# A two-block transformer kernel: the distance of moving tiles from the weights, a narrow panel turned round, and sums of squares token by token

## What is computed

```python
# first block, per layer
h = x @ w_in                       # 12 parts: q, k, v, gates, latents
cq, ckv = rmsnorm(b_cq), rmsnorm(b_ckv)
yc = rmsnorm(diff_attention(...))  # 4 heads of 128: a mean of squares per head and token
merged = ga * (ya @ w_a) + gb * (yb @ w_b) + gc * (yc @ w_c)
r = ALPHA * x + merged @ w_o
r = r + sigmoid(r @ w_pg) * (p_i @ w_p)
x = layernorm(r)
# second block, per layer
u = modulate(rmsnorm(h));  h += gate * swiglu(u, wg, wu, wd)      # width 2816
u = modulate(rmsnorm(h));  proj = u @ w_in                        # 5128 columns
# the last 8 columns of proj are mdt: dt = softplus(mdt + dt_bias), one per head of mamba
h += gate * (concat(retention, stick_breaking, mamba2) @ w_out)
u = modulate(rmsnorm(h));  h += gate * swiglu(u, ...)
```

## Time and profile before

| | |
|---|---|
| median of 3 runs | 2003.1 us (2002.36 to 2005.24) |
| the profiled execution | 2002.46 us, its span 2001.2 us |
| PE busy | 1893.1 us, 95%, 14952 matmul records |
| DVE busy | 1372.0 us, 69% |
| ACT busy | 954.4 us, 48% |
| mean granted TensorE clock | 0.978 |
| read from HBM | 386 MB, 194 GB/s over the span |

### The profile page before, as it was taken

One profiled execution on the slowest core, in us unless ns is written; L12 is line 12 of the kernel. 1 busy time (PEld: TensorE's weight loads), 2 busy tenths in 40 slices (PEclk: granted clock), 3 DMA queues, 4 the chain that ended last, 5 costly groups with the idle time before them and its releaser, 6 DMA issues.

```text
span 2001.2 us, 34162 instructions
## 1 busy us (share of the span) xinstructions
PE 1893.1 (95%) x14952; PEld 1819.0 (91%) x14952; DVE 1372.0 (69%) x1955; ACT 954.4 (48%) x1318; POOL 63.3 (3%) x76
## 2 busy tenths in 40 slices
PE   7998988899899898999999999999999999999998
PEld 7987888899788887999999889999999999799998
DVE  5667676666766767776775867767777776866555
ACT  5564454455644545434455435445444446344443
POOL 0000100000001001000000000001000000010000
PEclk9999999989999998999999999999999999999999
DMA  7453446464453554666455344665665455335551
GB/s 302 171 200 148 159 184 222 182 234 153 184 190 116 224 212 169 254 243 239 185 196 221 117 163 179 251 245 240 241 256 239 163 218 208 129 141 190 180 179 63
DMA packets 59285, 389.70 MB, mean 195 GB/s; under 512 B 6656, under 2 KB 9472, under 8 KB 15232
## 3 DMA queue, kind: packets, MB, share of 16 engines
q1 hardware_dynamic: 59136, 387.52, 50.6%
HBM read 386.45 MB, written 1.05 MB: 194 GB/s over the span
## 4 chain that ended last, share of the span: by engine, by line
PE 67%; DVE 21%; ACT 10%; issue 1%; DMA 0%; POOL 0%; SPq 0%; DVEq 0%; ACTq 0%
PE banks L753 17%; PE banks L754 16%; PE banks L755 16%; DVE weights_split L905 7%; PE bank L755 4%; PE bank L754 4%; PE bank L753 4%; ACT weights_split L899 4%; ACT map L1340 1%; DVE weights L885 1%; DVE xbc L2297 1%; DVE map_stat L1528 1%; ACT map L1346 1%; PE bank L820 1%; PE bank L831 1%
## 5 line engine op out<-in xcount | busy, mean ns | idle before, releaser
L905 DVE TENSOR_TENSOR weights_split<-weights,weights_split 128x2048 fp32r<-128x2048 f32 (+2 forms) x306 | 656.8, 2148 | 337.8 <-ACT weights_split L899 337.1
L753 PE MATMUL banks<-u,weights_split 128*128 128x258 f32 (+1 forms) x2016 | 578.3, 287 | 17.2 <-DVE weights_split L905 6.6
L899 ACT CAST weights_split<-weights 128x2048 fp32r<-128x2048 f32 (+2 forms) x306 | 542.5, 1775 | 80.2 <-PE bank L755 50.6
L754 PE MATMUL banks<-u,weights_split 128*128 128x258 f32 (+1 forms) x2016 | 575.6, 286 | 0.0
L755 PE MATMUL banks<-u,weights_split 128*128 128x258 f32 (+1 forms) x2016 | 572.5, 284 | 0.0
L753 PEld LDWEIGHTS banks<-u,weights_split 128*128 128x128 f32 x2016 | 384.6, 191 | 21.6 <-DVE weights_split L905 8.2
L755 PEld LDWEIGHTS banks<-u,weights_split 128*128 128x128 f32 x2016 | 387.9, 192 | 0.0
L754 PEld LDWEIGHTS banks<-u,weights_split 128*128 128x128 f32 x2016 | 386.3, 192 | 0.5 <-issue 0.5
L753 PE MATMUL banks<-x,weights_split 128*128 128x256 f32 x1056 | 302.9, 287 | 15.0 <-DVE weights_split L905 9.8
L754 PE MATMUL banks<-x,weights_split 128*128 128x256 f32 x1056 | 297.0, 281 | 0.0
L755 PE MATMUL banks<-x,weights_split 128*128 128x256 f32 x1056 | 296.9, 281 | 0.0
(11 more groups left out here) (320 smaller groups left out, 2561.1 us busy)
## 6 DMA issues: line engine op xcount, KB each, us to landing
weights<-in_weights SPq DMA_DIRECT2D x262, 1024.0 KB, 6.9
weights<-in_ada SPq DMA_DIRECT2D x80, 1024.0 KB, 4.8
weights<-in_weights SPq DMA_DIRECT2D x36, 512.0 KB, 5.5
weights<-in_weights SPq DMA_DIRECT2D x4, 576.0 KB, 5.3
constants_second<-in_constants_second SPq DMA_DIRECT2D x1, 1792.0 KB, 9.9
weights<-in_weights SPq DMA_DIRECT2D x2, 640.0 KB, 7.5
h<-in_x SPq DMA_DIRECT2D x2, 512.0 KB, 5.1
out<-xbc SPq DMA_DIRECT2D x4, 256.0 KB, 2.1
```

The costliest lines, as they stand in the source:

```text
L753: pe.matmul(out, left[0], right[0], start=start, stop=False, **more)
L754: pe.matmul(out, left[0], right[1], start=False, stop=False, **more)
L899: act.do.copy(split[:, 0, 0:n], raw[:, 0:n]).then_inc(*self.act_wrote.inc(("weights", key)))
L905: dve.do.tensor_tensor(split[:, 1, 0:n], raw[:, 0:n], split[:, 0, 0:n].bitcast(F32), ALU.subtract).then_inc(*self.dve_wrote.inc(("weights" ...
```

## The change

Three things are changed. First, a tile `space` of 128 bytes is put behind the split buffers, and the rows of `u` are made 384 elements (1536 bytes) long, of which 258 are used; the scratch for DMA descriptors shrinks from 16384 to 1024 bytes. Second, in `m_dt` the 8 columns of the panel are the stationary side and the 256 tokens move; ACT copies the 8 rows to SBUF, PE transposes them token-major (`turn_dt`) behind the first `s_q` panel, and `steps` comes after that. Third, the sums of squares are made token-major: the squares are stationary and one column of ones moves, so that each sum stands in its own row; DVE needs one small operation for all of them in place of the reduces, and the Newton step has one operation less.

```diff
+U_ROW = 384
@@ order of the mixers
         self.run(self.dense("m_dt", l, [0]))
-        self.add("steps", l)
...
         filler = Filler(fill())
+        filler.step()
+        self.add("turn_dt", l)
+        self.add("steps", l)
         filler.until("stick-breaking can start")
@@ tiles
         self.split = self.new_ring([self.tile(f"weights_split{i}", [P, 2, SLOT], F32R) for i in range(SPLIT_SLOTS)])
+        self.tile("space", [P, 32])
...
-        b["u_shift"] = sb("u", [P, DC, 2, T + 2], F32R)
-        b["u"] = b["u_shift"][:, :, :, 0:T]
+        u = sb("u", [P, DC, 2, U_ROW], F32R)
+        b["u_shift"], b["u"] = u[:, :, :, 0:T + 2], u[:, :, :, 0:T]
...
+        b["dt_rows"] = b["m_z"][0:MH, 0, :]
@@ tensor_norm
-            for g in range(0, groups, 2):
-                sums, some = ring.take(("sums", tag, g)), min(2, groups - g)
-                pe.wait_ge(*ring.free(("sums", tag, g)))
-                for k in range(chunks):
-                    pe.wait_ge(*wrote[k])
-                    rhs = squares[:, k, :] if groups == 1 else self.two(squares[:, g:g + 2, :])
-                    last = pe.do.matmul(sums[:, 0:some * T], self.k("ones"), rhs, start=k == 0, stop=k == chunks - 1)
-                last.then_inc(*self.filled.inc(("sums", tag, g)))
+            sums = ring.take(("sums", tag, 0))
+            pe.wait_ge(*ring.free(("sums", tag, 0)))
+            for k in range(chunks):
+                pe.wait_ge(*wrote[k])
+                for g in range(groups):
+                    for t in range(TB):
+                        col, square = g * TB + t, squares[:, g if groups > 1 else k, t * P:(t + 1) * P]
+                        last = pe.do.matmul(sums[:, col:col + 1], square, self.k("ones")[:, 0:1],
...
+            last.then_inc(*self.filled.inc(("sums", tag, 0)))
@@ vector_norm
-                dve.do.tensor_tensor_reduce(
-                    self.diagonal, sums[:, i * P:(i + 1) * P], self.k("ident"), 1.0 / count, eps, ALU.mult, ALU.add,
-                    mean[:, col:col + 1]).then_inc(*self.dve_wrote.inc(("mean", tag, g)))
...
+        dve.do.tensor_scalar(mean, ring.tile(("sums", tag, 0))[:, 0:n], 1.0 / count, eps, ALU.mult, ALU.add).then_inc(
+            *self.dve_wrote.inc(("mean", tag)))
...
-        dve.do.tensor_tensor(tmp, mean, inverse, ALU.mult).then_inc(*self.dve_wrote.inc())
+        dve.do.scalar_tensor_tensor(tmp, mean, -0.5, inverse, ALU.mult, ALU.mult).then_inc(*self.dve_wrote.inc())
...
-        dve.do.tensor_scalar(tmp, tmp, -0.5, 1.5, ALU.mult, ALU.add).then_inc(*self.dve_wrote.inc())
-        dve.wait_ge(self.dve_wrote, LAST)
-        dve.do.tensor_tensor(inverse, inverse, tmp, ALU.mult).then_inc(*self.dve_wrote.inc(("inverse", tag)))
+        dve.do.scalar_tensor_tensor(inverse, tmp, 1.5, inverse, ALU.add, ALU.mult).then_inc(
+            *self.dve_wrote.inc(("inverse", tag)))
@@ m_dt on PE
-            for j in range(TB):
-                tok = slice(j * P, (j + 1) * P)
-                for k in range(kc):
-                    last = self.parts(bank[:, j * MH:(j + 1) * MH], (t["u"][:, k, 0, tok], t["u"][:, k, 1, tok]),
-                                      (hi[:, k, :], lo[:, k, :]), k == 0, k == kc - 1)
+            for k in range(kc):
+                last = self.parts(bank[0:MH, 0:T], (hi[:, k, :], lo[:, k, :]), (t["u"][:, k, 0, :], t["u"][:, k, 1, :]),
+                                  k == 0, k == kc - 1)
@@ turn_dt on PE
+                for t in range(TB):
+                    last = pe.do.transpose(bank[:, t * MH:(t + 1) * MH], b["dt_rows"][:, t * P:(t + 1) * P],
+                                           self.k("ident")[0:MH, 0:MH])
@@ m_dt on ACT
+            act.do.copy(t["dt_rows"], bank[0:MH, 0:T]).then_inc(*self.act_wrote.inc(("dt_rows", l)))
+            self.products.emptied(bank_name, self.act_wrote, ("dt_rows", l))
@@ build
-    nc = bacc.Bacc("TRN2", target_bir_lowering=False, num_devices=1)
+    nc = bacc.Bacc("TRN2", target_bir_lowering=False, num_devices=1, dynamic_dma_scratch_size=1024)
```

More of the change, by code:

```diff
@@ L813, in tensor_norm @@
         if part == 0:
-            for g in range(0, groups, 2):
-                sums, some = ring.take(("sums", tag, g)), min(2, groups - g)
-                pe.wait_ge(*ring.free(("sums", tag, g)))
-                for k in range(chunks):
-                    pe.wait_ge(*wrote[k])
-                    rhs = squares[:, k, :] if groups == 1 else self.two(squares[:, g:g + 2, :])
-                    last = pe.do.matmul(sums[:, 0:some * T], self.k("ones"), rhs, start=k == 0, stop=k == chunks - 1)
-                last.then_inc(*self.filled.inc(("sums", tag, g)))
+            sums = ring.take(("sums", tag, 0))
[6 more added lines that the diff above has]
+                        last = pe.do.matmul(sums[:, col:col + 1], square, self.k("ones")[:, 0:1],
+                                            start=k == 0 and col == 0, stop=k == chunks - 1 and col == groups * TB - 1,
+                                            skip_group_check=True)
+            last.then_inc(*self.filled.inc(("sums", tag, 0)))
             return
@@ L846, in vector_norm @@
         dve.wait_ge(*self.stats.free(tag))
[L847 to L851, removed]
-                dve.wait_ge(self.dve_wrote, LAST)
-                dve.do.tensor_tensor_reduce(
-                    self.diagonal, sums[:, i * P:(i + 1) * P], self.k("ident"), 1.0 / count, eps, ALU.mult, ALU.add,
-                    mean[:, col:col + 1]).then_inc(*self.dve_wrote.inc(("mean", tag, g)))
-            ring.emptied(("sums", tag, g), self.dve_wrote, ("mean", tag, g))
+        dve.wait_ge(self.filled, ("sums", tag, 0))
+        dve.do.tensor_scalar(mean, ring.tile(("sums", tag, 0))[:, 0:n], 1.0 / count, eps, ALU.mult, ALU.add).then_inc(
+            *self.dve_wrote.inc(("mean", tag)))
+        ring.emptied(("sums", tag, 0), self.dve_wrote, ("mean", tag))
         dve.wait_ge(self.act_wrote, ("root", tag))
@@ L872, in scalar_norm @@
         st = self.stats.tile(tag)
-        self.act.wait_ge(self.dve_wrote, ("mean", tag, (groups - 1) // 2 * 2))
+        self.act.wait_ge(self.dve_wrote, ("mean", tag))
         self.act.do.activation(st[:, 2, 0:groups * TB], st[:, 0, 0:groups * TB], ACT.Sqrt).then_inc(
@@ L1793, in tensor_second @@
                 self.maps_t.emptied(("stick_map", l, i), self.filled, name)
+            elif what == "turn_dt":
+                l, = at
+                bank = self.scores.take(("turn_dt", l))
+                pe.wait_ge(self.act_wrote, ("dt_rows", l))
+                pe.wait_ge(*self.scores.free(("turn_dt", l)))
+                for t in range(TB):
+                    last = pe.do.transpose(bank[:, t * MH:(t + 1) * MH], b["dt_rows"][:, t * P:(t + 1) * P],
+                                           self.k("ident")[0:MH, 0:MH])
+                last.then_inc(*self.filled.inc(("turn_dt", l)))
             elif what == "decays":
@@ L2045, in scalar_second_bank @@
             self.scalar_tanh(key, t[name])
+        elif name == "m_dt":
+            act.wait_ge(self.filled, bank_name)
+            if l:
+                act.wait_ge(self.dve_wrote, ("y_r_out", l - 1, RH - 1))
+            act.do.copy(t["dt_rows"], bank[0:MH, 0:T]).then_inc(*self.act_wrote.inc(("dt_rows", l)))
+            self.products.emptied(bank_name, self.act_wrote, ("dt_rows", l))
         elif name in ("m_x", "m_bc"):
@@ L2373, in vector_steps @@
     def vector_steps(self, l):
-        dve, bank, dt_tile = self.dve, self.products.tile(("bank", ("m_dt", l, 0), 0)), self.b["dt"]
+        dve, bank, dt_tile = self.dve, self.scores.tile(("turn_dt", l)), self.b["dt"]
         z, lz, dt, da = (dt_tile[:, i, :] for i in (0, 3, 4, 5))
-        dve.wait_ge(self.filled, ("bank", ("m_dt", l, 0), 0))
+        dve.wait_ge(self.filled, ("turn_dt", l))
         for t in range(TB):
@@ L2380, in vector_steps @@
                 *self.dve_wrote.inc(("dt_in", l)))
-        self.products.emptied(("bank", ("m_dt", l, 0), 0), self.dve_wrote, ("dt_in", l))
+        self.scores.emptied(("turn_dt", l), self.dve_wrote, ("dt_in", l))
         dve.wait_ge(self.act_wrote, ("dt_log", l))
```

## The result

The kernel after takes 1988.3 us (median of four runs, 1984.97 to 1988.79) against 2002.7 for the kernel before beside it: a ratio of 0.9929, 95% interval 0.9915 to 0.9943. It is faster, by 14.4 us and not by the 31 of the forecast; the time lies in the range, near its upper end and 1 us from what the second rival (the distance does nothing) gave; that agreement is a coincidence, as the first experiment shows. The profiled execution of after took 1984.97 us, 17.5 less than that of before, so sums over the two traces come out 3 us larger than the medians.

What follows compares the result with a forecast made beforehand. TensorE, busy 95% of the span, was taken as the bound, above all in the feed-forwards. Terms 11.4 + 3.5 + 2.9 + 6.6 + 7 = 31.4 us off 2002.5 gave 1971 us, range 1936 to 1991.

Steps and rivals of the forecast that it cites:

- the second rival: Distance between weights and moving tiles does nothing; only m_dt and sums of squares gain, 13.6 us: 1989 us; chance 0.17.
- 1, u in the feed-forwards: 4224 u matmuls of 258 columns in the feed-forwards go from 119.8 to 117.1 ns: 11.4 us gained.
- The third rival: 192 bytes is a bad distance for full 128-column weight loads, so matmuls get slower: 2008 us; chance 0.08.
- parts 5 and 6: The terms for m_dt (6.6 us) and for the sums of squares in the norms (7 us), 13.6 us.
- 2 and 3: 256-column matmuls at 192 bytes: u in the mixers to 116.3 ns, 3.5 us; x, y, p, 2.9 us.
- 4, y2 at 0: 2112 y2 matmuls at an unchanged distance gain 0; 10.6 us if the low pace carries over from u.
- 5, m_dt: In two layers' mixers, m_dt takes 2.8 us and s_k starts 3.3 us earlier: 6.6 us, bounds 2 and 8.
- 6, norms: Sums of squares without DVE reduces shorten PE's waits, mainly at yc, r and m: 7 us, bounds -3 and 10.
- the fourth rival: One-column sums pull the clock down at eleven long norms, 2.9 us each, 31 us: back to 2002; chance 0.05.

Runs made afterwards that it cites:

- the first experiment: The kernel before with only the spare tile, the 384-element rows of u and the smaller DMA scratch: 1994.6 us, ratio 0.9960 (0.9949 to 0.9972).

## Why the prediction was off, step by step

**1, u in the feed-forwards: the step that failed.** It put 4224 matmuls from 119.8 to 117.1 ns, a gain of 11.4 us; they went up by 0.8 to 1.0 ns, a loss of 3.4. That is a miss of 14.8 us, where 14 (by the profiled runs) to 17 (by the medians) are missing in all; the misses of the other steps, -1.0, +5.9, -2.4 and -2.4 (the first two from one execution each), nearly cancel. The fault is in the choice of the row: 116.3 ns for the 96-column panel was 256 columns wide, and was carried over to 258 by adding 0.8 for two more columns. The width counts for more: at 192 bytes 256 columns have a pace of 113.3 open to them and 258 do not. The row was thin, too: nine matmuls, their starts 115 to 118 ns apart, and only one head in four stands at 192 (another at 448), not every second. Rows that had 258 columns were there, the chunks that the earlier trace rows shows six of (117 to 124 ns over the trace), and none of them at 192. The third rival (192 is a bad distance) was right for this shape, at half its price, and wrong for all others. The second rival's 1989 us is nearly the time measured, and its mechanism is false: the distance gave 8.0 us, and parts 5 and 6 gave 8.8 instead of its 13.6.

**2 and 3, 256 columns: mechanism right, sizes off.** The pace fell to 115.3 (u), 114.9 (x) and 115.3 (y) where 116.3 was forecast, and in the run with the weights moved x and u had the old pace again. It is a mix of 113.3 and 117.8, as the earlier trace rows had shown for x. In the first block I counted half of it on the path, 2.9 us; with distance alone 8.8 us came out (give or take 5, by the spread above). In the mixers I counted 60% of 5.8 for 2304 matmuls; in 384 of them u is the stationary side. With distance alone the mean of all of them fell by 4.1 ns, some 9 us of PE's time, and 2.5 us came out, less than 30%: as PE waits there in any case (78.9 of 85 us busy before), most of it is likely lost in longer waits, which was not followed wait by wait.

**4, y2 at 0:** right, 118.3 before, 118.4 after. The low pace did not carry over: at 224 bytes no more than 2% of a feed-forward's intervals were low in any run. y2 was also the part that could be had: 8.5 us for a spare tile.

**5, m_dt: 6.6 us forecast, 4.2 (2.0 to 6.4) measured.** 24 matmuls from 1007.22 on, done by 1010, as forecast. PE then, in the timeline of after (the bracket is PE's idle time before the instruction and what ended it; for the earlier trace rows):

```profile
1012.89 0.39 PE L757 MATMUL banks<-u,weights_split 128*128 128x256 f32 x1 [2.77 <-DVE weights_split L905]
...
1021.22 0.46 PE L757 MATMUL banks<-u,weights_split 128*128 128x256 f32 x1 [1.78 <-DVE weights_split L905]
...
1028.38 0.28 PE L757 MATMUL banks<-u,weights_split 128*128 128x256 f32 x1
```

The first row is s_q 0: PE has finished early and waits 2.8 us for its split. The third row is s_k. The second is s_q 1, 14.0 us behind m_dt's first matmul, and the prediction had 13.8. What it had not is the clock there, in the table by stage:

```profile
1021.40:1024.80 3.40, 3.40 (x17) 3.40 (x18) 3.32 (x5) 0.05 (x1) 0.00 (x0) 0.50 0.28 87
1024.80:1028.40 3.60, 3.60 (x34) 3.60 (x34) 0.10 (x1) 3.51 (x7) 0.00 (x0) 1.00 1.01 428
```

The half-speed stretch did not go with m_dt's one-sided matmuls; behind PE's new waits it fell into s_q 1, 17 matmuls in 3.4 us instead of some 30. So s_k starts 21.2 us behind m_dt's first matmul instead of the 19.5 forecast, against 22.8 before. In layer 1 it is 20.7 against 23.0: there 17 matmuls of s_q 0 ran at half speed, and s_q 1 began 14.9 us behind m_dt.

**6, norms: 7 us forecast, 4.6 (2.4 to 6.8) measured.** The waits did go. PE's waits in the run with the sums alone (us in total, times, longest):

```profile
PE bank L834 <- DVE statistics L861: 11.4, 9, 1.9
```

and in the kernel before, for the same wait and for one behind the reduces:

```profile
PE bank L831 <- DVE statistics L866: 19.7, 11, 2.8
...
PE bank L1128 <- DVE statistics L853: 2.3, 2, 1.1
```

That is 10.6 us less, more than was forecast. Part of it is lost in two ways. The sums themselves are no cheaper: 32 one-column records, 112 ns from start to start, where 16 records had 216 ns each (3.6 us against 3.5), and for yc and r 16 of them where 4 had 429 ns (1.8 against 1.7). And the clock falls earlier, the fourth rival. The norm of mix, 18 us from its first sum, before and then with the sums alone:

```profile
984.60:1002.60 18.00, 14.41 (x81) 13.03 (x80) 13.52 (x32) 9.13 (x16) 0.00 (x0) 0.81 0.13 52
```

```profile
982.10:1000.10 18.00, 15.09 (x96) 14.28 (x96) 12.92 (x28) 9.18 (x16) 0.00 (x0) 0.72 0.14 54
```

The factors' four matmuls behind them are at half speed then, on PE's timeline of each (before, then sums alone), with the wait in front shorter:

```profile
990.26 0.71 PE L831 MATMUL bank<-constants,statistics 128*128 128x128 f32 x4 [1.95 <-DVE statistics L866]
```

```profile
987.23 1.22 PE L834 MATMUL bank<-constants,statistics 128*128 128x128 f32 x4 [1.27 <-DVE statistics L861]
```

Over the trace the clock stood at half speed for 123 us, in the kernel before for 90, and 411 split matmuls have 180 to 235 ns to the next start, where 353 had; at some 96 ns more each, that is an estimated 5.6 us. The mean granted clock was 0.969 to 0.974 in all ten executions and 0.975 to 0.982 in the 21 of before. The fourth rival's mechanism exists, then, at a price of a few us and not of its 31. How much of it one run has varies (the run with the distance alone has 397 such matmuls), so what it costs here is known to a few us only: 10.6 less 5.6, and less some 1 us for the sums, is near the 4.6 measured.

**The rule of the Trainium skill** that the moving operand and the weight load have read ports of their own and that PE never waits on anyone (TensorE: Matmul & The Clock Gate, Part 2, "Step-by-step"; SBUF — State Buffer, "Who interferes with whom") leaves no room for a price of their distance; the traces show one: 113.6 against 118.4 ns for y2 by 32 bytes of distance, and 117.4 when only the weights were moved. Which of the memory's or the engine's parts does it, no run here shows.

## What to carry to other kernels

Measure a dense matmul stream from start to start, per shape and per distance between the moving tile and the weights, before a price is carried from one shape to another; two columns more can turn the best distance into one of the worst. Where two paces exist for one instruction, see what runs just before the stream as well as where its tiles lie, and judge the pair: u and y2 together were worth the same at 64 and at 16 bytes, though each had its own favourite. When a step is made shorter, ask where the half-speed stretch that stood in it goes, and whether the operand of the next step is there.

## What the runs showed of the hardware

- A stream of fp32r matmuls (128x128 weights, 256 columns) has two steady paces at full clock, 113.3 and 117.8 ns. At 192 and 448 bytes mod 512 between weights and moving tile both occur (in the kernel after the low one in 64% of x's intervals and 54% of y's); at 64 and 320 bytes the high one mostly (the low one in 17% of x's in the kernel before); at 176 and 224 bytes the mean is 119.0 and 118.4 and the low pace isn't held (at most 4% of a feed-forward's intervals).
- A stream settles on one of the two within its first ten or so matmuls and nearly always keeps it to its end (none of the 800 stretches of y2 in the twenty traces changed after its twelfth matmul, two of x's 45 in the kernel before did), and which one depends on where the stream in front lies: y2 at 192 bytes was at 113.6 ns behind 258 columns at 64 bytes in four of four feed-forwards, and at 117.3 to 117.7 behind 16 bytes in four of four, as the mean of each. It isn't the pace of the stream in front that is taken over: u of 256 columns at 192 bytes was at 114.0 behind y2 at 117.8. That a start phase is what is handed on fits the repeating intervals, but is argued, not shown; the runs with 264 columns speak against its simplest form.
- Moving tiles of 258 to 272 columns never held a low pace: 116.8 to 122.2 ns for 258, 118.4 to 120.9 for 260, 120.0 to 123.4 for 264, 123.4 for 272.
- In the kernel before eight of the sixteen parts of u began 8 bytes off a multiple of 16. If the time to the next start is booked on the matmul in front, four of them were the slowest of all, 123.0, 122.8, 123.9 and 123.0 ns at 88, 120, 136 and 152 bytes (the other four 119.0 to 121.6), against 117.2 to 120.5 at the multiples of 16. Booked on the matmul behind, the order is another (128 and 144 bytes slowest, 121.7), so that the 8 bytes cost is not shown.
- Plain fp32 matmuls with 128x128 weights have 112 ns from record to record (two records each) at one moving column and 216 at 256; fp32r ones have 111 ns at 8 columns and 113.3 at 256 at best. So one column for 256 saves half in plain fp32, and 8 for 256 save next to nothing in fp32r. What sets this floor, no run here separates.
